# The entry of the gated layer: earlier sums and splits of the first weight blocks, the second up tile last

## The reference

```
x = x + mixed @ w_out
h2 = rmsnorm(x, norm_ffn_g)
gate = causal_dwconv(h2 @ w_gate, ffn_conv_w) + ffn_conv_b     # 3 taps over the tokens
x = x + (silu(gate) * (h2 @ w_up)) @ w_down                    # D_FF = 2816
return rmsnorm(x, norm_final_g)
```

## Time and profile before

| | |
|---|---|
| median of 3 runs | 1390.34 us (1389.62 to 1392.69) |
| the profiled execution | 1392.53 us, its span 1390.7 us |
| granted clock of TensorE, mean | 0.986 |
| PE busy | 1318.5 us (95%) |
| DVE busy | 863.5 us (62%) |
| ACT busy | 576.2 us (41%) |
| POOL busy | 332.6 us (24%) |

### The profile page before, as it was taken

How to read it: one execution, slowest core, us unless ns; L and a number is a source line. 1 busy time by engine, 2 the same in 40 slices (tenths; PEclk the granted TensorE clock), 3 DMA queues, 4 the chain that set the end, 5 groups by cost and what they waited for, 6 DMA issues and landing times.

```text
span 1390.7 us, 17095 instructions
## 1 busy us (share of the span) xinstructions
PE 1318.5 (95%) x6366; PEld 1076.2 (77%) x6366; DVE 863.5 (62%) x1195; ACT 576.2 (41%) x1028; POOL 332.6 (24%) x248
## 2 busy tenths in 40 slices
PE   7999999988888899889997999999999999999996
PEld 6788888876667687768886788888888878888885
DVE  6433352179887888654458888877777873345442
ACT  6211121078777787532353333333333332234330
POOL 0100100033131321100065455545445410001010
PEclk9999999999999999999999999999999999999998
DMA  5111112000000000143112222122222248435631
GB/s 220 53 45 45 61 46 91 0 20 1 1 1 1 1 2 1 49 169 131 63 40 80 91 74 75 64 91 91 74 78 92 76 157 298 157 118 167 202 97 61
DMA packets 37965, 110.75 MB, mean 80 GB/s; under 512 B 4016, under 2 KB 4528, under 8 KB 37680
## 3 DMA queue, kind: packets, MB, share of 16 engines
q1 hardware_dynamic: 37552, 108.83, 22.4%
q0 software_dynamic: 336, 0.90, 0.3%
HBM read 90.01 MB, written 19.92 MB: 79 GB/s over the span
## 4 chain that ended last, share of the span: by engine, by line
PE 74%; DVE 13%; issue 6%; ACT 5%; POOL 1%; DMA 1%; DVEq 0%; SPq 0%; ACTq 0%; POOLq 0%
PE PS L496 9%; PE PS L497 8%; PE PS L500 8%; PE PS L2037 6%; PE PS L2039 6%; PE PS L2038 6%; PE PS L2049 6%; PE PS L2051 6%; PE PS L2050 6%; PE PS L1902 3%; DVE wl L1560 3%; ACT F L1053 2%; PE PS L1919 2%; DVE nmax L1439 2%; PE PS L1854 2%
## 5 line engine op out<-in xcount | busy, mean ns | idle before, releaser
L496 PE MATMUL PS<-R,wh 128*128 128x512 f32 x560 | 222.7, 398 | 13.7 <-DVE wl L488 13.7
L497 PE MATMUL PS<-R,wh 128*128 128x512 f32 x560 | 219.7, 392 | 0.0
L2037 PE MATMUL PS<-R,wh 128*128 128x512 f32 x480 | 189.3, 394 | 13.6 <-DVE wl L1560 8.4
L2038 PE MATMUL PS<-R,wh 128*128 128x512 f32 x480 | 188.1, 392 | 0.0
L2039 PE MATMUL PS<-R,wl 128*128 128x512 f32 x480 | 187.9, 392 | 0.0
L500 PE MATMUL PS<-R,wl 128*128 128x512 f32 x560 | 173.8, 392 | 0.0
L2049 PE MATMUL PS<-R,wh 128*128 128x512 f32 x352 | 137.5, 390 | 0.0
L2051 PE MATMUL PS<-R,wl 128*128 128x512 f32 x352 | 137.0, 389 | 0.0
L2050 PE MATMUL PS<-R,wh 128*128 128x512 f32 x352 | 137.0, 389 | 0.0
L496 PEld LDWEIGHTS PS<-R,wh 128*128 128x128 f32 x560 | 106.3, 190 | 37.6 <-DVE wl L488 14.6
L497 PEld LDWEIGHTS PS<-R,wh 128*128 128x128 f32 x560 | 106.3, 190 | 22.5 <-issue 0.7
(11 more groups left out here) (222 smaller groups left out, 2442.6 us busy)
## 6 DMA issues: line engine op xcount, KB each, us to landing
raw<-in_w_units SPq DMA_DIRECT2D x70, 512.0 KB, 3.6
F<-in_w_units SPq DMA_DIRECT2D x32, 512.0 KB, 4.1
gated<-F SPq DMA_DIRECT2D x22, 512.0 KB, 2.6
F<-gated SPq DMA_DIRECT2D x44, 256.0 KB, 3.6
F<-in_xT SPq DMA_DIRECT2D x16, 512.0 KB, 9.2
F<-in_w_units SPq DMA_DIRECT2D x12, 384.0 KB, 3.1
residual<-F SPq DMA_DIRECT2D x8, 512.0 KB, 2.6
F<-residual SPq DMA_DIRECT2D x8, 512.0 KB, 6.2
```

The lines of the kernel that those rows point to most:

```text
L496: nc.tensor.matmul(out, w_h, hi(kt)[:, cols], start=first, stop=False)
L497: nc.tensor.matmul(out, w_h, lo(kt)[:, cols], start=False, stop=False)
L2037: nc.tensor.matmul(out, w_h, operand(name, k, 0), start=fresh and k == 0, stop=False, skip_group_check=not fresh)
L2038: nc.tensor.matmul(out, w_h, operand(name, k, 1), start=False, stop=False, skip_group_check=not fresh)
```

## The change

The four sums of matrix 0 get places of their own instead of the right halves of the tiles that hold B22 and the raw T2: S1 and S2 in the two halves of F1's tile 4 (the accumulator of the squares, free once the norm's sums have been taken, hence the wait for `ss_ready`), S3 and S4 behind RB in PBm. The waits of matrix 0's sums for the token-side work fall away; matrix 1's first sum takes them over.

On POOL, S1 and S2 come ahead of the first `spread_silu`, S3 and S4 behind it and ahead of the four combinations T4. On ACT and DVE the split of A11 comes ahead of the T3 splits, those of S2 and S1 ahead of the second gate tile's steps, that of S3 behind them. On DVE `first_up(0)` comes behind the T3 splits instead of ahead of them, and `first_up(1)` behind the T4 splits instead of ahead of them. SP's and PE's queues are as they were.

```diff
@@ def block_of(m, name)
+            if name[0] == "S" and m == 0:
+                return (F1[:, 4, LEFT], F1[:, 4, RIGHT], PBm[:, 1024:1024 + BANK], PBm[:, 1024 + BANK:2048])[int(name[1]) - 1]
             if name[0] == "S":
                 return F1[:, X1 + 4 + int(name[1]) - 1, RIGHT]
@@ POOL, def sum_of(m, j)
-                if m:
+                if m > 1:
                     pool.wait_ge(p_lo, NP * (m - 1) + [name for name, _ in PRODUCTS].index(f"S{j}") + 1)
-                elif j == 1:
+                elif m and j == 1:
                     pool.wait_ge(t_lo, 2 * 4)
                     pool.wait_ge(t_made, 4 * 4)
+                elif j == 1:
+                    pool.wait_ge(ss_ready, 3)
@@ POOL
+            for j in (1, 2):
+                sum_of(0, j)
             pool.wait_ge(rn_ready, 1)
             spread_silu(1, 0)
+            for j in (3, 4):
+                sum_of(0, j)
             for k in range(4):
                 combine("T4", k, t_raw("T2", k), ALU.subtract, b21(k), 8 + k + 1)
-            for j in range(1, 5):
-                sum_of(0, j)
             spread_silu(2, 1)
@@ ACT
                 split_t("T2", k)
+            split_product(0)
             silu(1, 0)
             for k in range(4):
                 split_t("T3", k)
+            split_product(1)
+            split_product(2)
             tap(1, 1, 2)
-            for n in range(4):
-                split_product(n)
+            split_product(3)
             silu(2, 1)
@@ DVE
                 split_t("T2", k)
-            first_up(0)
+            split_product(0)
             for k in range(4):
                 split_t("T3", k)
+            first_up(0)
+            split_product(1)
+            split_product(2)
             first_gate(1)
             taps(2, 1, 1, 2)
-            for n in range(4):
-                split_product(n)
-            first_up(1)
+            split_product(3)
             for k in range(4):
                 split_t("T4", k)
+            first_up(1)
```

## The result

| | before | after |
|---|---|---|
| median of 8 runs each, taken together | 1391.22 us (1389.62 to 1392.91) | 1395.36 us (1394.06 to 1397.21) |
| ratio, 95% interval | | 1.003 (1.0021 to 1.004) |
| the profiled execution, its span | 1392.53, 1390.7 us | 1394.73, 1392.9 us |
| PE, DVE, POOL busy | 1318.5, 863.5, 332.6 us | 1317.5, 868.4, 334.3 us |

The changed kernel is slower by 4.1 us, and the whole interval lies above 0.2%. Forecast: 1394.7, from 1388.3 to 1398.0.

What follows compares the result with a forecast made beforehand. The request of matrix 1's blocks was taken to bound the kernel, not PE's start. Request +5.7, store +0.3, clock -1.6 gave +4.4 us: 1394.7 us from the median 1390.34, range 1388.3 to 1398.0.

Steps and rivals of the forecast that it cites:

- What binds: Layer's start: the request of matrix 1's blocks (749.30) sets the time from 781.70 on; PE's start has little weight.
- The turns on DVE: DVE splits beside POOL's sums: engines alternate, 0.6 us DVE and 1.12 POOL; first product at 740.8 instead of 741.79.
- DVE isn't held: Faster rival, DVE splits: they pass in POOL's pauses, load 4.1 us earlier, 1384.6 to 1386.2 us; chance 12%.
- The request, +5.7: SP's load of matrix 1's blocks: goes at 755.0 instead of 749.30, 5.7 us later.
- the second up tile comes last: DVE and SP ahead of matrix 1's load: its 1.15 us and the store join the chain, given as the later request's cost.
- The store, +0.3 with bounds 0 and 1.3: Store just ahead of matrix 1's load: lengthens the landing by 0.3 us, bounds 0 and 1.3.
- PE's stop in front of product 6, 5.5 us: PE in matrix 0: idles 5.5 us until C22, product 6 near 766; nothing waits for that.
- my three signs of being wrong: Profile after: load at or before 750, no PE stop before product 6, or another chain shape from 760 to 787.
- The other two: Remaining signs of being wrong: SP's load at or before 750; another chain shape from 760 to 787.
- The clock, -1.6: Behind matrix 1's product 6: idle time and slow matmuls vanish, giving back 1.6 us, bounds 0 and 1.6.
- +4.4: Whole kernel: summed change in us, 5.7 for the request, 0.3 for the store, less 1.6 for the clock.
- my estimate for e4: Experiment's forecast with engines taking turns: load 2.1 us later than before's, +0.5 to +2.1 us against before.

Runs made afterwards that it cites:

- e1: Changed kernel with SP's load of matrix 1's blocks ahead of the second tile's store; median +3.6 us against before, ratio 1.0026.
- e4: Kernel before with only the new orders on ACT and DVE, sums' places and POOL's order as before; median +4.6 us against before, ratio 1.0032.
- e5: Kernel before, with F1/PBm space given to matrix 1's blocks, loaded early, and U2 ahead of T4's splits; median -2.3 us against before, ratio 0.9979.
- e6: Changed kernel with e1's load order and U2 ahead of the second up tile on DVE; median +2.7 us against before, ratio 1.0016.
- e3: Changed kernel's sum places and POOL order, with ACT's and DVE's orders of before; median +2.1 us against before, ratio 1.0011.
- e2: Changed kernel with the second up tile ahead of the T4 splits again on DVE; median +3.5 us against before, ratio 1.0023.
- e8: Changed kernel run again unchanged; median +5.6 us against before, ratio 1.0033.
- e10: Changed kernel with matrix 1's load ahead and the second tile's store behind matrix 2's gate-block load; median +1.9 us against before, ratio 1.0018.
- e9: e5 with POOL's order of before and DVE's and ACT's splits reordered for an early PE start; 1386.99 us, -4.0 against before, ratio 0.9972.
- e7: e5 plus an early PE start, S1 and S2 of matrix 0 in the raw weights' third slot; median -1.3 us against before, ratio 0.9986.

## Why the prediction was right, step by step

- **What binds.** Right. The chain runs through the request; product 6 of matrix 1 stood 27.0 us behind S1 in eight kernels. e1 (start of product 3 unchanged, end moved), e4 (PE's start 8.6 us earlier, kernel slower), e5 (PE's start unchanged, kernel faster) and e6 (product 3 moved, end unmoved against its landing) tell it apart from PE's own stops.
- **The turns on DVE.** Right in kind: T2 took 7.98 us, the first product started 2.0 us earlier on the common clock (22.61 against 24.60; I had 1.0), released by `first_up(0)`. In size the T2 splits took 7.98 where I had walked 8.6 (732.0 less 723.4), the T3 splits 5.69, near the 5.8 walked. The rival "DVE isn't held" is refuted by T2 alone, and e3 prices the cause: +1.95 us for the earlier sums.
- **The request, +5.7.** The mis-sized term: 36.63 less 32.11 is +4.5. On before's clock the taps ended at 745.98 (745.04 plus 0.94) and not 747.05, most of it from the cheaper T2 splits, and POOL's long product took 2.41 us and not 2.8. The T4 splits were held as walked: they ended 2.35 us behind that product (750.97 less 748.62), walked 2.5. Against that, 0.75 us instead of 0.33 passed between SP's issue of the store and that of the load. And its cause was given too narrowly, as "the second up tile comes last". With the load no longer behind up tile and store (e1) 2.6 of the 4.5 stay, and the sums alone cost 1.95 (e3); the up tile back in its old place gives only 0.5 (e2).
- **The store, +0.3 with bounds 0 and 1.3.** In the first trace 0.2 (5.60 less 5.39). In e8 it was 1.96, outside the bound. The Trainium skill's rule of ring order (DMA: Bandwidth & Descriptors, Queues, rings and completion order) agrees with the rows under e10: the store's bytes go first. But the 1.3 that I drew from it was wrong, for they are through before the load's own would begin. No run shows a cost of the store by itself; what was left out is the spread of the transfer, up to 2.0 us.
- **PE's stop in front of product 6, 5.5 us.** Wrong. It was 5.03 us and in front of product 3, since `sum_u2(0)` stands behind the second up tile on DVE; I had looked at the weight operand's split and C22 and not at U2. With the slow clock behind that stop (starts 0.43 apart, from 754.58 to 759.27) product 5 ends at 764.88, 1.0 us after C22 (763.87), and PE has nothing to wait for there. It changed nothing in the sum, because that stretch is off the path (e6). "PE doesn't stop in front of product 6" was one of my three signs of being wrong, and it came true in the first trace (in e8 PE stops there 1.72 us). It was a bad sign to choose: it strikes the order of PE's stops, which I held to have no weight, and not the chain. The other two didn't come: on before's clock the load went at 753.8, and the chain kept its shape.
- **The clock, -1.6.** In the first trace right: no slow matmul behind 785.50, though 1.42 us of idle time stayed where I had none. In e8 it was there again. In these two traces it is worth 1.6 us or nothing.
- **Sum.** From the first trace 4.74 less 1.6 is +3.1, and the spans with the common points taken out give the same (1392.9 plus 0.94 less 1390.7 is 3.1). e8 gives +6.4 less 0. The medians, +4.1 and +5.6, lie between. So the direction and the cause were right, and that +4.4 came within 0.3 of the first median is in part luck: the request was 1.2 too dear, the transfer too cheap by up to 1.7, and the clock's 1.6 came in one trace of two.

## What to carry to other kernels

Look first for the transfer or result that the chain hangs on at the far end of the stretch, and price a change by how it moves the request of that; a shorter or longer stop of PE ahead of it said nothing here, even as the largest new one in the list of waits (e6), and an earlier start of PE by 8.6 us went with a slower kernel (e4). An idle engine that shares its access with a busy one is not free room: four sums made earlier, two of them in POOL's idle time, cost DVE 2 us on the path (e3). If there is a spare home in SBUF, give it to the data whose load has to wait for space (e5, e9), not to results that already have one.

## What the runs showed of the hardware

- DVE and POOL do not always take turns. Single subtractions of both alternate at 1.72 us a pair, but five DVE splits whose inputs were ready ran at 0.6 us each and kept a POOL product of 1024 columns out (5.25 us instead of 2.77, e4). The Trainium skill, SBUF — State Buffer, section SBUF: two separate sides, has the lock for a whole instruction, with which both rows agree; who gets it next was what my estimate for e4 missed.
- The same load took 5.34 to 7.35 us from issue to use, within one kernel 5.60 to 7.35. A store of 512 KB issued 0.75 us ahead of it on the same queue had its bytes through first, and the load's came at full rate 2.4 us behind its issue with that store or without (rows under e10).
- The lower clock (1.2 GHz of the two levels) came behind idle times of 1.83 us (before), 1.81 (e3) and 1.79 (e8), and did not behind 2.27 (e7), 1.81 (e6), 1.80 (e4) and 1.79 (e9) at the same product. The length of the idle time alone doesn't decide it; what does, these runs don't show.
